# Fifteen projection tiles in five slots of three, with the gates' stage woven between them

## The reference, cut to what matters

```python
h = rms_norm(x, norm_mix[l])
p_rw, p_s5, p_gla, p_gate = _split(h @ w_in[l], IN_SIZES)
...
def rwkv7_mix(p, mu, w0, w_up, a0, a_up, g_up, k_k, k_a, r_k, ln_w, ln_b):
    p = p + (_token_shift(p) - p) * mu
    r, k, v, wd, ad, gd = _split(p, RWKV_SIZES)       # 512, 512, 512, 64, 64, 128
    w_log = -jax.nn.softplus(-(w0 + jnp.tanh(wd) @ w_up)) - 0.5
    a = jax.nn.sigmoid(a0 + ad @ a_up)
    g = jax.nn.sigmoid(gd) @ g_up
    kk = heads(k * k_k)
    kk = kk * lax.rsqrt(jnp.sum(kk * kk, axis=-1, keepdims=True) + 1e-12)
    k = k * (1 + (a - 1) * k_a)
    decay = jnp.exp(-jnp.exp(heads(w_log)))
    ...                                               # recurrence over the 512 tokens
```

## Time and profile before

| what | us |
|---|---|
| median of three runs (3801.19 to 3808.68) | 3805.7 |
| the profiled execution, whole | 3807.16 |
| its span | 3805.2 |
| TensorE busy in the span | 3333.2 (88%) |
| VectorE busy | 1556.3 (41%) |
| ScalarE busy | 1140.6 (30%) |
| mean granted TensorE clock | 0.922 |

### The profile page before, as it was taken

One profiled execution on the slowest core, in us unless ns is written; L12 is line 12 of the kernel. 1 busy time (PEld: TensorE's weight loads), 2 busy tenths in 40 slices (PEclk: granted clock), 3 DMA queues, 4 the chain that ended last, 5 costly groups with the idle time before them and its releaser, 6 DMA issues. The chain is left out here.

```text
span 3805.2 us, 49050 instructions
## 1 busy us (share of the span) xinstructions
PE 3333.2 (88%) x19354; PEld 2482.1 (65%) x19354; DVE 1556.3 (41%) x2458; ACT 1140.6 (30%) x1694; POOL 535.4 (14%) x394
## 2 busy tenths in 40 slices
PE   7688867888799889998868789999998999979998
PEld 5365521565546568776647577888555888838877
DVE  5444269222123456622265532221003788723432
ACT  2312254121311233223355532221002455423321
POOL 0000012000010234315012221000003222200001
PEclk9899878995799999998989798999998999999999
DMA  3276100120023022222100011111112111112222
GB/s 134 90 267 228 56 36 0 66 90 0 22 88 122 28 83 88 97 76 71 61 1 1 1 45 45 66 64 41 59 46 90 51 67 67 62 66 89 88 83 83
DMA packets 30423, 268.43 MB, mean 71 GB/s; under 512 B 2848, under 2 KB 5280, under 8 KB 10144
## 3 DMA queue, kind: packets, MB, share of 16 engines
q1 hardware_dynamic: 30240, 265.88, 19.2%
HBM read 261.68 MB, written 4.19 MB: 70 GB/s over the span
## 5 line engine op out<-in xcount | busy, mean ns | idle before, releaser
L595 PE MATMUL banks<-normed_high,weights_high 128*128 128x512 f32 (+1 forms) x2272 | 855.1, 376 | 121.0 <-DVEq L547 64.6
L595 PE MATMUL banks<-normed_low,weights_high 128*128 128x512 f32 (+1 forms) x2272 | 847.7, 373 | 0.0
L595 PE MATMUL banks<-normed_high,weights_low 128*128 128x512 f32 (+1 forms) x2272 | 846.3, 372 | 0.0
L595 PEld LDWEIGHTS banks<-normed_high,weights_high 128*128 128x128 f32 x2272 | 437.5, 193 | 226.5 <-DVEq L547 72.7
L261 DVE TENSOR_TENSOR weights_low<-ring,weights_high 128x1024 fp32r<-128x1024 f32 (+1 forms) x195 | 270.0, 1385 | 641.8 <-ACTq L534 631.9
L532 ACT ACTIVATE weights_high<-ring 128x1024 fp32r<-128x1024 f32 (+1 forms) x239 | 278.3, 1165 | 784.8 <-PE banks L595 478.6
L595 PEld LDWEIGHTS banks<-normed_high,weights_low 128*128 128x128 f32 x2272 | 437.8, 193 | 73.9
L595 PEld LDWEIGHTS banks<-normed_low,weights_high 128*128 128x128 f32 x2272 | 438.6, 193 | 69.8
L564 POOL TENSOR_TENSOR latent_total<-latent_total,latent_square 128x512 f32<-128x512 f32 x42 | 77.2, 1838 | 1591.3 <-ACTq L517 1591.3
L595 PE MATMUL banks<-ffn_hidden,ring 128*128 128x256 f32 (+1 forms) x704 | 227.3, 486 | 1.1 <-PEq L152 1.1
L2781 PE MATMUL banks<-normed_high,hg_weights_high 128*128 128x512 f32 (+1 forms) x512 | 189.7, 370 | 15.1 <-DVEq L451 15.1
(11 more groups left out here) (534 smaller groups left out, 4915.8 us busy)
## 6 DMA issues: line engine op xcount, KB each, us to landing
ring<-in_ffn_up SPq DMA_DIRECT2D x33, 2048.0 KB, 8.1
ring<-in_ada SPq DMA_DIRECT2D x48, 1024.0 KB, 7.0
ring<-in_ffn_down SPq DMA_DIRECT2D x24, 1408.0 KB, 6.0
ring<-in_hgrn SPq DMA_DIRECT2D x16, 1536.0 KB, 6.5
ring<-in_gates SPq DMA_DIRECT2D x6, 2048.0 KB, 8.3
ring<-in_wo SPq DMA_DIRECT2D x6, 2048.0 KB, 8.3
ring<-in_w_rw SPq DMA_DIRECT2D x4, 2048.0 KB, 11.0
ring<-in_branch SPq DMA_DIRECT2D x3, 2048.0 KB, 8.0
```

Source lines behind the costliest of these rows:

```text
L595: mm = pe.matmul(ps[:, 0:y.shape[-1]], w, y, start=(kk == 0 and n == 0), stop=(kk == kt - 1 and n == len(pairs) - 1))
```

## The change

- The padding of 240 zero columns shrinks to 112, so that there are 15 tiles, in five slots of three tiles (1.5 MB each). Each section that comes later lies in the other half of the ring and starts in another accumulator bank than before.
- The tiles are taken in the order `RW_SLOTS`: the low-rank columns first (12, 13, 14), then the keys (4 to 7), then r (0 to 3) and v (8 to 11).
- The gates' stage is gone as a stage. `linear` calls `aside["tensor"]` behind each tile's matmuls, `aside["scalar"]` behind `high` of the next tile, and `aside["vector"]` behind a tile's eviction; the instructions of the gates' stage stand there, by tile number n.
- The Ln of all four key norms is taken before the Exp of all four, and the sums of squares go to banks 4 to 7.
- `one_less_mu` is computed at the end of the input stage.
- The clearing of the SiLU window stands at the start of the projection stage, on GpSimd. `rw_up` is fetched at its start, modulation groups 2 and 3 when 12 tiles are ready, groups 0 and 1 when all 15 are.
- `rw_up`, the low-rank inputs, the norm's root and scaled pieces lie in buffers that exist for other uses (`mixer_out`, `rw_norms`).

```diff
-SECTIONS = [("w_rw", 4, 4096), ("gates0", 2, 4096), ("branch0", 1, 4096),
+RW_SLOTS = (12, 13, 14, 4, 5, 6, 7, 0, 1, 2, 3, 8, 9, 10, 11)
+SECTIONS = [("w_rw", 5, 3 * DT * P), ("gates0", 2, 4096), ("branch0", 1, 4096),
...
+                if then is not None:
+                    then(sp, lay)
...
+                        if aside and part == lay.nparts - 1:
+                            aside["tensor"](pe, s * tiles + j)
...
+                            if name == "scalar" and aside:
+                                aside["scalar"](e, s * tiles + j)
...
+                            if name == "vector" and aside:
+                                aside["vector"](e, s * tiles + j)
...
+            v.wait_ge(inputs_loaded.sem, 32)
+            v.tensor_scalar(k.one_less_mu[:], k.vec("mu", 0, 16), -1.0, 1.0, ALU.mult, ALU.add).then_inc(e.sem, e.tick())
...
-            OM = k.sb("one_less_mu", [P, 16], s1)
...
-                    v.tensor_scalar(OM[:], k.vec("mu", 0, 16), -1.0, 1.0, ALU.mult, ALU.add).then_inc(e.sem, e.tick())
...
-            linear(k, "w_rw", [k.H.operand(LAT)], shift, per=2, keep_free=2, norms=[lead])
...
-            rwkv_gates(k, PR, A, G, KK, LD, GKD, CW)
+            rwkv_inputs(k, PR, A, G, KK, LD, GKD, CW, Y, norm_of)
...
+    LOW, WS = Y[:, 0:2, :], Y[:, 2:4, :]
...
+        def by_scalar(e, n):
+            a = e.eng
+            if n == 1:
...
                                  ACT.Silu).then_inc(e.sem, e.tick())
+            if n == 3:
+                a.wait_ge(evicted.sem, evicted.base + 3)
+                a.wait_ge(fetched.sem, fetched.at(16))
...
-                a.sem_inc(squashed.sem, 1)
+                a.sem_inc(low_ready.sem, 1)
+            if 5 <= n < 5 + MT:
+                t = n - 5
+                a.wait_ge(made.sem, made.at(3 * t + 1))
+                a.activation(LD[:, t, :], k.PS[4][:], ACT.Sigmoid, bias=k.vec("w0", t)).then_inc(e.sem, e.tick())
+                a.wait_ge(made.sem, made.at(3 * t + 2))
+                a.activation(A[:, t, :], k.PS[5][:], ACT.Sigmoid, bias=k.vec("a0", t)).then_inc(e.sem, e.tick())
+                a.wait_ge(made.sem, made.at(3 * t + 3))
+                a.activation(G[:, t, :], k.PS[6][:], ACT.Copy).then_inc(e.sem, e.tick())
+                a.wait_ge(e.sem, e.now())
...
+            if n == 9:
+                a.wait_ge(lead.ready.sem, lead.ready.at(DT))
+                a.wait_ge(weighted.sem, weighted.at(MT))
...
                     a.activation(N[:, t, :], KK[:, t, :], ACT.Square).then_inc(e.sem, e.tick())
...
+                a.wait_ge(e.sem, e.now())
+                a.sem_inc(squared.sem, 1)
+            if n == 10:
                 for t in range(MT):
...
-                    inverse_root(e, N[:, t, :], k.PS[t][:], 1.0, k.eps[1e-12])
...
+                    a.activation(N[:, t, :], k.PS[4 + t], ACT.Ln, bias=k.eps[1e-12][:]).then_inc(e.sem, e.tick())
+                a.wait_ge(e.sem, e.now())
                 for t in range(MT):
-                    if t:
-                        pe.wait_ge(taken.sem, taken.at(t))
-                    c = slice(t * P, t * P + P)
-                    pe.matmul(k.PS[4][:], WS[0:64, 0, c], LOW[0:64, 0, :]).then_inc(made.sem, 1)
-                    pe.matmul(k.PS[5][:], WS[64:P, 0, c], LOW[64:P, 0, :]).then_inc(made.sem, 1)
-                    pe.matmul(k.PS[6][:], WS[:, 1, c], LOW[:, 1, :]).then_inc(made.sem, 1)
+                    a.activation(N[:, t, :], N[:, t, :], ACT.Exp, scale=-0.5).then_inc(e.sem, e.tick())
+                a.wait_ge(e.sem, e.now())
+                a.sem_inc(rooted.sem, 1)
...
+        def by_tensor(pe, n):
+            if 4 <= n < 4 + MT:
+                t = n - 4
+                if t == 0:
+                    pe.wait_ge(low_ready.sem, low_ready.at(1))
+                else:
+                    pe.wait_ge(taken.sem, taken.at(t))
+                c = slice(t * P, t * P + P)
+                pe.matmul(k.PS[4][:], WS[0:64, 0, c], LOW[0:64, 0, :]).then_inc(made.sem, 1)
+                pe.matmul(k.PS[5][:], WS[64:P, 0, c], LOW[64:P, 0, :]).then_inc(made.sem, 1)
+                pe.matmul(k.PS[6][:], WS[:, 1, c], LOW[:, 1, :]).then_inc(made.sem, 1)
+            if n == 9:
+                pe.wait_ge(taken.sem, taken.at(MT))
+                pe.wait_ge(squared.sem, squared.at(1))
...
+                    pe.matmul(k.PS[4 + t], k.const("pair"), N[:, t, :]).then_inc(made.sem, 1)
+
+        def by_vector(e, n):
+            v = e.eng
+            if 3 <= n < 3 + MT:
+                t = n - 3
+                v.tensor_scalar(KK[:, t, :], PR[:, 4 + t, :], k.vec("k_k", t), None, ALU.mult).then_inc(e.sem, e.tick())
+                v.wait_ge(e.sem, e.now())
+                v.sem_inc(weighted.sem, 1)
+            if 7 <= n < 7 + MT:
...
+                v.wait_ge(taken.sem, taken.at(t + 1))
...
+                v.tensor_tensor_scan(PR[:, 12 + t, :], k.const("reset", 0, L), LD[:, t, :], 0.0,
...
+                v.tensor_tensor(LD[:, t, :], PR[:, 12 + t, :], LD[:, t, :], ALU.subtract).then_inc(e.sem, e.tick())
...
+            if n >= 11:
+                t = n - 11
+                v.wait_ge(rooted.sem, rooted.at(1))
+                v.tensor_tensor(KK[:, t, :], KK[:, t, :], N[:, t, :], ALU.mult).then_inc(e.sem, e.tick())
...
+                v.tensor_scalar(N[:, t, :], A[:, t, :], -1.0, k.vec("k_a", t), ALU.add, ALU.mult).then_inc(e.sem, e.tick())
...
+                v.scalar_tensor_tensor(PR[:, 4 + t, :], N[:, t, :], 1.0, PR[:, 4 + t, :], ALU.add, ALU.mult).then_inc(e.sem, e.tick())
+                v.tensor_tensor(A[:, t, :], KK[:, t, :], A[:, t, :], ALU.mult).then_inc(e.sem, e.tick())
+                v.wait_ge(e.sem, e.now())
...
+        def fetch(sp):
+            sp.dma_start(WS, k.dram["rw_up"]).then_inc(fetched.sem, 16)
+
+        def then(sp, lay):
+            sp.wait_ge(k.tile_ready.sem, lay.t0 + 12)
+            for n in (2, 3):
+                ada_load(k, sp, n)
+            sp.wait_ge(k.tile_ready.sem, lay.t0 + 15)
+            for n in (0, 1):
+                ada_load(k, sp, n)
+
+        def clear(g):
+            g.memset(CW[:], 0.0).then_inc(cleared.sem, 1)
+        linear(k, "w_rw", [k.H.operand(LAT)], shift, tiles=3, per=2, keep_free=2, norms=[lead], fetch=fetch, then=then,
+               aside=dict(scalar=by_scalar, tensor=by_tensor, vector=by_vector, gpsimd=clear),
+               more=dict(low_ranks_ready=1, products_ready=4 * MT, operands_ready=MT, window_cleared=1, keys_weighted=MT,
+                         key_squares_ready=1, key_roots_ready=1, small_weights_loaded=16))
...
-    d["w_rw"] = slots(np.concatenate([rw, gkd, np.zeros((D, 240), np.float32)], axis=1), 4)
+    rw = np.concatenate([rw, gkd, np.zeros((D, 112), np.float32)], axis=1).reshape(D, len(RW_SLOTS), P)
+    d["w_rw"] = slots(rw[:, RW_SLOTS].reshape(D, -1), 3)
```

122 lines of the change are left out of this document (33 added, 89 removed).

## The result

The changed kernel takes 3771.28 us (median of four runs, 3770.61 to 3780.62), the kernel before 3807.19 beside it on the same chip: a ratio of 0.991, with a 95% interval of 0.9898 to 0.9923. It is faster, by about 36 us. The forecast was 3768.5 with a range of 3762 to 3779. Run again beside other kernels, the same kernel took 3778.79 (median of five) against 3809.32, a ratio of 0.9917; the last row of the table of the experiments has it.

A forecast was written before the change was run, and what follows sets the result against it. TensorE was taken to bound the projection, with a chain of waiting engines behind it. Start 15.9 + tiles 97.1 + products 11.7 + stalls 0.6 + end 4.9 = 130.2 against 167.5, giving 3768.5 us, range 3762 to 3779.

The forecast's parts named there:

- The start: First `high` of the projection waits 1.2 us less for its smaller slot, starting at 15.9 us.
- Tiles and products: Projection on TensorE: fifteen tiles take 97.13 us, woven products and sums of squares add 11.7.
- ScalarE: Woven work between projection tiles costs nothing; heaviest piece 9.4 us, `high` of tiles 5 and 12 0.3 late, harmlessly.
- VectorE: Nearly full windows between projection tiles: TensorE waits 0.3 us before tiles 13 and 14, 0.6 in all.
- The first rival: VectorE becomes the bound of tiles 9 to 14, 1 us over in six windows: 6 us back, 3774.5; chance 0.12.
- The end: Behind tile 14, eviction, four VectorE instructions and barrier take 4.9 us; modulation fetch hidden.
- The clock at the chunk stage: TensorE's clock at the chunk stage's start: taken as 0, between 2.9 us gained and 1.5 lost.
- Later stages: Stages behind the projection use the other ring half and another bank: cost taken as 0.
- the third rival: A later stage that was in step with something loses, say, half of the gain: 3787 us; chance 0.03.
- Slower, because nothing overlaps: Every woven piece between projection tiles runs alone, TensorE waiting over 45 us: 3818 us; chance 0.03.

The follow-up runs named there:

- the slots alone: Kernel before with only fifteen tiles in five slots of three, gates' stage still its own stage: 3801.6 us, ratio 0.9982.
- the grouped roots: Kernel before, gates' stage unwoven, with only all four Ln put ahead of all four Exp: 3809.76 us, one run.
- the reordered kernel: Changed kernel with `low` ahead of woven instructions, two three-instruction groups behind tile 9, four-instruction groups one tile earlier; with 18 matmuls 3772.15 us, without 3771.56.
- the sixteen tiles: Changed kernel's weaving, but sixteen tiles in four slots, padding tile fourth, keys weighted one tile later: 3779.97 us, ratio 0.9926.
- the late slots: Changed kernel with slots 2 to 4 fetched two tiles later: 3789.21 us, one run.
- the order with 18 and with 6 matmuls: Changed kernel with `low` first and woven groups moved earlier, plus 18 or 6 unread matmuls behind tile 14: 3772.15 and 3772.41 us.

## Why the prediction came out right, and where it was off

Point by point, measured against predicted:

- **The start:** the wait for the first slot is 1.22 us shorter (predicted 1.2); the experiment on the slots alone has the same 2.85.
- **Tiles and products:** from `high` of tile 0 to the last matmul 109.36 us; 97.13 + 11.7 + 0.6 = 109.4 was predicted. Before tiles 5 to 8 the distances are 7.71 to 7.72 (I said about 7.6), before tile 10 9.03 (9.1). So the products and sums took 4 x 2.12 + 3.43 = 11.9 us, 0.2 more than the 11.7, and the first two tiles were 0.1 shorter than before; that the total agrees to 0.1 us is in part such small errors cancelling.
- **ScalarE:** never late. Its heaviest piece took 102.08 - 93.70 = 8.4 us, not the 9.4 of the text. I had priced eight activations at 0.72 each by the squares of the earlier trace rows; there each waited for the one ahead of it, and here four go one behind the other in 2.19 (Exp) or 2.43 (Ln). With the waits between them, in the grouped roots above, four Exp took 2.89 again. The 0.3 us by which `high` of tile 12 was to be late did not come, nor did the 0.3 for tile 5 (at 51.66 ScalarE had been idle for 0.18 us), and no term of the sum hung on them.
- **VectorE:** 0.55 us of stalls in all, 0.6 predicted. The windows came out full as worked out, but the stalls lie otherwise: I had two of 0.3 before tiles 13 and 14 and held that the window with three woven instructions just fits. Measured are 0.18 us behind such a window, before tile 12, and 0.12 and 0.25 behind those with four. The first rival failed by its size (the windows are over by 0.1 to 0.25 us, not by 1), not by its mechanism: 0.69 us more in a window cost 0.64.
- **The end:** 4.85 us (4.9). Exponentials at 130.35 (130.2). The modulation's first matmuls start at 135.12, 4.8 us into the stage, and wait for no DMA, as predicted.
- **The clock at the chunk stage:** I took 0 between -2.9 and +1.5. It fell again and came back a pair of groups earlier in the stage's life: the first copy of `rwc_n2t` comes 138.18 - 130.35 = 7.83 us after the exponentials, and before it was 8.57. But the changed kernel run again has 7.08 there, and the experiments without more matmuls lie between 7.14 and 8.65. So the value 0 was right within the spread of single executions, but not for my reason. I had read from one fall that the clock falls 4.7 us into an idle time and that 5.1 us are just long enough. It fell 4.7 us in once more in the changed kernel's first execution, but 2.0 us in its second, after 3.5 and 3.3 in the slots alone and the grouped roots, and with 1.0 us of idling, where the copy came after 7.42, it fell all the same. So the fall has no fixed distance from the last matmul, and that the sum was right with 0 is luck.
- **Later stages:** I took 0. By one pair of traces that holds: 3637.7 us and 3639.5 us from the exponentials to the end, and together with the 0.25 us by which the spans start apart, 37.37 - 0.25 - 1.7 is the 35.4 us between the profiled executions. The last `gate`, some 900 us later, is 36.8 us ahead of before:

```profile
L804 ACT ACTIVATE gate<-banks x24: 597/598/598, 403.7 to 1045.9; 128x512 f32<-128x512 f32 x24
```

```profile
L822 ACT ACTIVATE gate<-banks x24: 597/598/601, 365.6 to 1009.1; 128x512 f32<-128x512 f32 x24
```

The row begins with its line, engine and count, and ends with first and last start: 403.7 to 365.6 is 38.1 ahead, 1045.9 to 1009.1 is 36.8. So the gain is made in the projection and kept, against the third rival in the form in which I gave it. But the step was priced from one execution, and here it was least sure. In the nine compared runs of the changed kernel the median is 3776.9, some 32 us below the 3808.8 of the thirteen runs of the kernel before beside them, and not 36. That the first comparison came out 3 us from the forecast is therefore in part luck: the second, 3778.79, lies at the very end of the range. Two traces of the very same kernel show where that goes, a stretch near the middle (columns as above):

```profile
1830.00:1880.00 50.00, 36.62 (x177) 24.54 (x176) 20.96 (x30) 29.41 (x34) 0.00 (x0) 0.93 0.14 53
```

```profile
1832.00:1882.00 50.00, 38.16 (x172) 25.89 (x172) 17.59 (x26) 27.58 (x32) 0.00 (x0) 0.81 0.14 53
```

Nearly the same work, with the granted clock at 0.93 in one and 0.81 in the other: a `low` ahead of it starts 2.2 us later in the second execution (1826.18 against 1823.99), and an instruction at its end 5.6 us later (1880.99 against 1875.39). It shows in what comes behind; in each row of the tile `pa_turned` (duration min, median, max, then first and last start)

```profile
L2381 PE MATMUL banks<-pa_turned,gq_values x896: 272/273/477, 1916.6 to 2160.4; 128*64 128x128 f32 x180
```

```profile
L2381 PE MATMUL banks<-pa_turned,gq_values x896: 272/273/477, 1922.3 to 2168.4; 128*64 128x128 f32 x180
```

the first start is 907.5 us behind the last `gate` in the one (1916.6 - 1009.1) and 912.5 in the other (1922.3 - 1009.8). Of the thirteen profiled executions six have 904.1 to 907.6 there, among them the kernel before and the two edits of it, and seven, all of woven kernels, 912.4 to 913.0. The third rival, 18 us in my text, is thus alive at some 5 us (my estimate: 37.4 by the stage less 32 by the runs), with the clock as its likely cause. Whether woven kernels fall into the longer course more often because of where their stages come to lie, or by chance, stays open: the interval of the first comparison holds the full 37 us (a ratio of 0.9902), that of the second begins just above it.
- **Slower, because nothing overlaps:** refuted; TensorE waited 1.0 us.

## What to carry to other kernels

Work that waits on several engines costs little more than its time on the bound engine (here 11.9 us of TensorE in place of a stage of 46) between the tiles of a stage that this engine bounds, as long as each window of the second-busiest engine is added up with all that stands in it: here VectorE's windows were over by 0.1 to 0.25 us, and one instruction more cost nearly its whole length, except where other work in the bound engine's stream gave cover. In a full window put first what the bound engine waits for: the same instructions behind `low` instead of ahead of it gave back the stall. A fixed gain in a stage should be read from the trace, since in the total time of a kernel whose TensorE clock comes and goes it can hide behind several microseconds of clock.

## What the runs showed of the hardware

- The time of the changed kernel goes with its mean granted clock: of its nine compared executions the four at 0.924 to 0.926 took 3770.6 to 3774.3 us, the five at 0.921 to 0.923 took 3776.9 to 3780.6. The kernel with `low` first had 0.922 in its one run, and 3781.36 us with a stage that is 0.51 us shorter.
- With 18 matmuls behind tile 14 the clock fell at 132.7 us although TensorE had worked without a break until 129.61 and then idled for only 1.0 us; behind it came 1.12 us of matmuls and 1.51 us without any. In the reordered kernel with the same 18 matmuls, whose chunk stage begins 0.9 us earlier, it did not fall, and in the changed kernel run again it was back at 133.6 us, where the first execution had it back at 137. So a single execution can't price an edit by this term. The Trainium skill ("TensorE: Matmul & The Clock Gate", section "What's actually happening") says that "the default state is throttled, and activity releases the throttle"; that the slow groups of the changed kernel end only after TensorE has worked nearly without a break from 133.22 to 136.98 agrees with it.
- The same chance shows in the unwoven gates' stage: two kernels that left its products as they were lost 1.9 us in the second tile of them. It shows at tiles 0 and 1 too: in four of the ten profiled executions of woven kernels the granted clock went to 0.50 there for some 3 us (the sixteen tiles, the late slots, the order with 18 and with 6 matmuls), in six it stayed at 1.00, though nothing that these kernels differ in had run by then but the size of the first slot.
- A slot of 1.5 MB landed 6.6 us after its issue (median), one of 2 MB 8.5.
